# Loading each expert's weights as eight sets of one or two chunks in place of twelve transfers

## The reference, cut to what matters

```python
def moe(h, router_w, router_b, w1, b1, w2, b2):        # h: [512, 1024]
    top_v, top_i = lax.top_k(h @ router_w + router_b, 4)   # 4 of 32 experts for each token
    top_w = jax.nn.softmax(top_v, axis=-1)
    ...
    def block_ffn(args):                                # a block of tokens of one expert
        tok, e = args
        z = h[tok] @ w1[e] + b1[e]                      # w1[e]: [1024, 2048] float32, 8 MB
        z_glu, z_lin = jnp.split(z, 2, axis=-1)
        ...                                             # clamps
        act = z_glu * jax.nn.sigmoid(1.702 * z_glu) * (z_lin + 1.0)
        return act @ w2[e] + b2[e]                      # w2[e]: [1024, 1024] float32, 4 MB
```

## Time and profile before

| | |
|---|---|
| median of 3 runs | 1591.79 us (1590.99 to 1595.43) |
| span of the profiled execution | 1584.0 us |
| what the median has beside that span | 7.8 us |
| TensorE busy | 1461.9 us, 92% of the span |
| VectorE, ScalarE, GpSimd busy | 46%, 16%, 13% |
| moved by DMA | 497.19 MB, mean 314 GB/s |
| expert weights | 384 transfers of 1 MB, 204 into `big_b`, 180 into `arena` |

### The profile page before, as it was taken

The page is one execution under the profiler, slowest core; times in us unless marked ns, Lnnn a source line. Parts: engine busy times, 40 slices in busy tenths (PEclk is TensorE's granted clock), DMA queues, the critical chain, the costliest instruction groups (busy, mean ns, idle before and its releaser), DMA issues.

```text
span 1584.0 us, 39651 instructions
## 1 busy us (share of the span) xinstructions
PE 1461.9 (92%) x14639; PEld 738.5 (47%) x14639; DVE 735.8 (46%) x2464; ACT 261.3 (16%) x467; POOL 210.6 (13%) x267
## 2 busy tenths in 40 slices
PE   5999999999896899999979999979899979999896
PEld 3658888888653333433323434323333424333232
DVE  4503877777638544443424434424343423434244
ACT  4402555555413200000000000000000000000001
POOL 1000000000051112111211111211121111212110
PEclk9999999999998999999989999979999979999798
DMA  9685211112577999998798999999799998998997
GB/s 388 192 265 148 62 54 53 53 53 57 172 306 274 358 413 407 412 415 347 301 415 339 408 417 417 414 414 417 321 417 416 417 414 321 410 417 344 413 400 295
DMA packets 130857, 497.19 MB, mean 314 GB/s; under 512 B 15356, under 2 KB 48476, under 8 KB 94892
## 3 DMA queue, kind: packets, MB, share of 16 engines
q1 hardware_dynamic: 122396, 479.93, 77.1%
q0 software_dynamic: 8256, 16.81, 2.8%
q10 hardware_dynamic: 176, 0.06, 0.0%
HBM read 484.92 MB, written 17.58 MB: 317 GB/s over the span
## 4 chain that ended last, share of the span: by engine, by line
PE 71%; DMA 15%; SPq 7%; DVE 4%; issue 1%; ACT 1%; ACTq 0%; DVEq 0%; POOLq 0%
PE ps L1838 28%; PE ps L1870 14%; DMA big_b<-in_moe_w 7%; PE ps L1541 6%; PE ps L1542 6%; PE ps L1543 6%; DMA arena<-in_moe_w 5%; SPq L431 4%; PE ps L1720 3%; SPq L425 2%; PE ps L1652 1%; PE ps L1564 1%; DMA arena<-in_final_g 1%; PE ps L1851 1%; PE ps L1666 1%
## 5 line engine op out<-in xcount | busy, mean ns | idle before, releaser
L1838 PE MATMUL ps<-arena,rows 128*32 128x512 f32 x2736 | 318.2, 602 | 26.7 <-DMA arena<-in_moe_w 20.1
L1838 PE MATMUL ps<-big_b,rows 128*32 128x512 f32 x2688 | 316.8, 607 | 21.8 <-DMA big_b<-in_moe_w 21.8
L886 ACT ACTIVATE rows<-ps 128x256 f32<-128x256 f32 x84 | 32.3, 385 | 977.0 <-issue 661.5
L1838 PEld LDWEIGHTS ps<-arena,rows 128*32 128x32 f32 x2736 | 86.8, 111 | 214.0 <-issue 159.2
L1838 PEld LDWEIGHTS ps<-big_b,rows 128*32 128x32 f32 x2688 | 85.5, 111 | 208.1 <-issue 153.3
L1870 PE MATMUL ps<-big_b,rows 128*32 128x256 f32 x2688 | 163.9, 395 | 8.1 <-DMA big_b<-in_moe_w 8.1
L1870 PE MATMUL ps<-arena,rows 128*32 128x256 f32 x2688 | 161.7, 392 | 9.3 <-DMA arena<-in_moe_w 8.5
L1434 DVE SCALAR_TENSOR_TENSOR y_sb<-ps,w_s,g_q 128x256 f32<-128x256 f32 x42 | 20.3, 484 | 261.0 <-PE ps L1870 261.0
L1434 DVE SCALAR_TENSOR_TENSOR rows<-ps,w_s,g_q 128x256 f32<-128x256 f32 x42 | 20.3, 484 | 256.8 <-PE ps L1870 256.8
L1870 PEld LDWEIGHTS ps<-big_b,rows 128*32 128x32 f32 x2688 | 84.2, 113 | 68.1 <-DMA big_b<-in_moe_w 12.9
L1870 PEld LDWEIGHTS ps<-arena,rows 128*32 128x32 f32 x2688 | 84.1, 112 | 67.0 <-DMA arena<-in_moe_w 13.0
(11 more groups left out here) (360 smaller groups left out, 1785.0 us busy)
## 6 DMA issues: line engine op xcount, KB each, us to landing
big_b<-in_moe_w SPq DMA_DIRECT2D x204, 1024.0 KB, 14.2
arena<-in_moe_w SPq DMA_DIRECT2D x180, 1024.0 KB, 15.4
ring_t<-in_hg_w_in SPq DMA_DIRECT2D x32, 512.0 KB, 3.9
ogT<-in_mod_w SPq DMA_DIRECT2D x16, 1024.0 KB, 5.0
arena<-yrows SPq DMA_DIRECT2D x8, 1024.0 KB, 12.6
x_sb<-in_x SPq DMA_DIRECT2D x2, 2048.0 KB, 7.9
arena<-in_hg_w_in SPq DMA_DIRECT2D x4, 1024.0 KB, 13.8
arena<-in_mod_c SPq DMA_DIRECT2D x4, 1024.0 KB, 19.7
```

The source lines that it names most:

```text
L1838: last = mm(bank[q * G:(q + 1) * G, :], XT[par][:, pos * G:(pos + 1) * G], w[:, :, q * NW:(q + 1) * NW], start=(pos == 0), stop=False)
```

## The change

The weights keep their size and their total, but lie otherwise in HBM. w1 of an expert is laid out in five sets: chunk 0, chunks 1 and 2, chunk 3, chunks 4 and 5, chunks 6 and 7. w2 is laid out in three sets: chunks 0 and 1, chunk 2, chunk 3. Within a set, what one partition gets is one run: 8 KB in a set of one chunk, 16 KB in a set of two. Before, a partition's run was 8 KB for w1 and 4 KB for w2 (two runs in each chunk). The host writes the weights in this order ahead of the launch. Each set is one transfer with one semaphore; TensorE waits ahead of a set's first chunk and not ahead of its second; SP issues a set when TensorE has used the last chunk of the old set. The two chunks of a set must stand side by side in SBUF, so `B1_AT` and `B2_AT` change.

```diff
+W1_SET = ((0, 1), (1, 3), (3, 4), (4, 6), (6, 8))
+W2_SET = ((0, 2), (2, 3), (3, 4))
...
-        B1_AT, B2_AT = (5, 6, 7, 10, 11, 2, 3, 4), (0, 1, 8, 9)
+        flat_b = big_b[:, :, :].rearrange("p s n -> p (s n)")
+        B1_AT, B2_AT = (5, 6, 7, 4, 10, 11, 2, 3), (0, 1, 9, 8)
...
-            def load_w1(par, e, pos):
-                sp.dma_start(w1_slot(par, pos), moe_w1[bass.ds(e * D + pos * P, P), :]
-                             ).then_inc(ld_w1[par][pos], 16)
...
+            def load_set(par, e, at_a, at_b, source, sems, first, last):
+
+                n = (last - first) * 2 * FF
+                to = arena[:, at_a:at_a + n] if par == 0 else flat_b[:, at_b * 2 * FF:at_b * 2 * FF + n]
+                rows = source.rearrange("(r a) n -> r (a n)", a=last - first) if last - first > 1 else source
+                sp.dma_start(to, rows[bass.ds(e * (source.shape[0] // E // (last - first)) + first * P // (last - first), P), :]
+                             ).then_inc(sems[par][first], 16)
...
-                    over_w1(0, AHEAD)
+                    over_w1(range(4))
                     with sp.If(new_next):
-                        for k in range(W2C):
-                            sp.wait_ge(S["w2_used"], i * (2 * W2C) + (par * W2C + k + 1))
-                            load_w2(1 - par, e_next, k)
+                        for j in range(3):
+                            sp.wait_ge(S["w2_used"], i * (2 * W2C) + (par * W2C + W2_SET[j][1]))
+                            load_w2(1 - par, e_next, j)
...
-                    over_w1(AHEAD, W1C)
+                    over_w1(range(4, 5))
...
-                pe.wait_ge(ld_w1[par][pos], count + 16 * (1 - par))
+                if pos in (0, 1, 3, 4, 6):
+                    pe.wait_ge(ld_w1[par][pos], count + 16 * (1 - par))
...
-                    pe.wait_ge(ld_w2[par][m], i * 16 + 32)
+                    if m != 1:
+                        pe.wait_ge(ld_w2[par][m], i * 16 + 32)
```

More of the change, by code:

```diff
@@ L422, in _, with load_w1, load_w2 @@
                 sp.dma_start(b_raw[part * E:(part + 1) * E, :], moe_b1).then_inc(S["ld_br"], 16)
-            def load_w1(par, e, pos):
-                sp.dma_start(w1_slot(par, pos), moe_w1[bass.ds(e * D + pos * P, P), :]
-                             ).then_inc(ld_w1[par][pos], 16)
[L428 to L432, removed]
+            def load_set(par, e, at_a, at_b, source, sems, first, last):
[4 more added lines that the diff above has]
+                             ).then_inc(sems[par][first], 16)
+            def load_w1(par, e, j):
+                first, last = W1_SET[j]
+                load_set(par, e, first * 2 * FF, B1_AT[first], moe_w1, ld_w1, first, last)
+            def load_w2(par, e, j):
+                first, last = W2_SET[j]
+                load_set(par, e, 16384 + first * 2 * D, B2_AT[first], moe_w2, ld_w2, first, last)
             def store(i):
@@ L438, in store @@
                 sp.dma_start(hrows[i * P:(i + 1) * P, :], x_sb[:, i, :]).then_inc(S["h_st"], 16)
-            for pos in (5, 6, 7, 1, 2):
-                load_w1(1, 1, pos)
+            for j in (4, 2, 1):
+                load_w1(1, 1, j)
             sp.wait_ge(S["a_ps"], H)
-            for pos in range(W1C // 2):
-                load_w1(0, 0, pos)
+            for j in range(3):
+                load_w1(0, 0, j)
             sp.wait_ge(S["o_ps"], H)
             sp.wait_ge(S["og_ok"], H)
-            for pos in range(W1C // 2, W1C):
-                load_w1(0, 0, pos)
+            for j in range(3, 5):
+                load_w1(0, 0, j)
             sp.wait_ge(S["bias_ok"], 1)
@@ L453, in _ @@
             sp.wait_ge(S["yo_ps"], 2 * LT)
-            for k in range(2):
-                load_w2(0, 0, k)
+            load_w2(0, 0, 0)
             store(LT - 1)
             sp.wait_ge(S["lg_ps"], LT)
-            for pos in range(3, 5):
-                load_w1(1, 1, pos)
-            load_w2(0, 0, 2)
+            load_w1(1, 1, 3)
+            load_w2(0, 0, 1)
             sp.wait_ge(S["h_st"], 16 * LT)
             sp.wait_ge(ld_xg[0], 16)
-            for k in range(2):
-                load_w2(1, 1, k)
+            load_w2(1, 1, 0)
             for n in range(2):
                 sp.wait_ge(frow[n], 16 * (LT // 2))
-            load_w2(1, 1, 3)
+            load_w2(1, 1, 1)
             sp.wait_ge(S["late_free"], 1)
-            load_w2(0, 0, 3)
+            load_w2(0, 0, 2)
             sp.wait_ge(S["ring_free"], 1)
@@ L1942 @@
           "router_w": [D, E], "router_b": [E], "moe_w1": [E * D, 2 * FF], "moe_b1": [E, 2 * FF],
-          "moe_w2": [E * FF, D], "moe_b2": [E, D]}
+          "moe_w2": [E * FF // 2, 2 * D], "moe_b2": [E, D]}
 def kernel(**inputs):
@@ L1956 @@
     for name, n in (("moe_w1", 2 * FF), ("moe_w2", D)):
-        laid[name] = np.asarray(inputs[name]).reshape(E, QT, DK, G, n).transpose(0, 2, 1, 3, 4)
+        a = np.asarray(inputs[name]).reshape(E, QT, DK, G, n).transpose(0, 2, 1, 3, 4).reshape(E, DK, P, n)
+        sets, per = (W1_SET, 1) if name == "moe_w1" else (W2_SET, 2)
+        laid[name] = np.concatenate([a[:, first * per:last * per].transpose(0, 2, 1, 3).reshape(E, -1)
+                                     for first, last in sets], axis=1)
     for name in INPUTS:
```

21 lines of the change are left out of this document (11 added, 10 removed).

## The result

The changed kernel takes 1595.47 us in the median of 20 runs (1591.76 to 1600.06), the kernel before 1591.39 us (20 runs, 1584.41 to 1597.49). The ratio is 1.0033, 95% interval 1.0021 to 1.0045: **slower by a third of a per cent, where 0.44% faster was forecast.** 1595.47 us lies inside the range, at its far end. A second set of twelve runs gave 1.0029 (1.0010 to 1.0047).

A forecast was written before the change was run, and what follows sets the result against it. Bound: mostly TensorE's products, plus late weights in episodes paced by the DMA queue. Gains of 9.2 us, less 1.0 for half clock and 1.2 for gathers, gave 7.0 us: 1584.8 us, 0.44% faster; range 1578 to 1596 us.

The forecast's parts named there:

- Longer runs: Weight loads in the DMA queue: runs of 8 and 16 KB save 0.48 us a load, 1.6%.
- the list: Expert-stage episodes between queue dry points: gains of 1.4, 1.05, 3.85, 2.4, 0, 0, and 0.5 at the end, together 9.2 us.
- Coarser waits: TensorE's stalls ending on a set's second chunk: 0.86 us later each, plus 0.5 us for half clock at two places.
- Coarser release: SP's issue of a set of two comes 0.86 us later, but the queue holds over 2 us of work: no cost.
- The gathers at the start: Two token gathers on the chain at the start: held longer by longer runs, 0.6 us each, 1.2 us in all.
- The time around the span: Time of a run outside the profiled span: 7.8 us, which the change doesn't touch.
- Fewer instructions: Four TensorE waits fewer a block, four SP transfers fewer a load: no gain, though SP had 7% of the chain.
- the undisturbed block: A block of the expert stage in which TensorE doesn't wait: should still cost 10.87 us.
- no gain in pace: Rival on the weight loads: only 0.24 us or 0 saved a load, counted as no change; chance 0.30.
- zero case: Part of the no-gain rival: run length saves 0 us a load, giving 1594 to 1596 us; chance 0.12.
- its sign: What would show no gain in pace: in a stall, a set of two takes 4.98 us or more.
- Late gathers: Rival on block gathers: landing up to 9.5 us against 8.1 of room, 84 us lost, 1669 us; chance 0.10.

The follow-up runs named there:

- both edits: TensorE's waits and SP's releases go by the eight sets, still twelve 1 MB transfers, against w2 in 8 KB runs; ratio to before 1.0050 (1.0029 to 1.0071).

## Why the prediction was wrong

The pace came as predicted; the step that failed is the price of the coarse sets, waits and release together: 5.3 us in the sum, 13 us measured (both edits over w2 in 8 KB runs). A second one is what the pace was to give in time. The terms in their order:

- *Longer runs*, 0.48 us a load: right where the queue is dense. A set of two took 4.89 us (1505.90 to 1510.79 above; 4.92 predicted), a single w2 2.48. What a packet pays whatever its length is 11 to 12 ns by the medians above (two of 8 KB less one of 16, two of 4 less one of 8), where 7.5 was taken. The Trainium skill's "DMA: Bandwidth & Descriptors" (Specifications), by which 4 and 8 KB would run alike, is not borne out between those two, by 0.07 us a MB. But the list turned 1.6% of pace into 9.2 us net of 4.3 us for the coarse waits, so **13.5 us gross, which failed too**: measured is 3.3 us for the step to 8 KB and 0.4 to 4.1 us for that to 16 KB, behind the first blocks, where one kernel's two profiles lie as far apart. Over long stretches of full queue the changed kernel moved 0 to 1% more, not 1.6%.
- *Coarser waits*: **the step that failed, in the size of its term.** 0.86 us at each end on a set, and 0.5 for the clock at two places, 5.3 us in all; every such wait had a lowered clock behind it (0.50 in most, 0.62 at the highest measured), 1.9 us each, and coarse waits alone cost 7.6 us by the times. The ends on w2 chunk 3, where nothing was to be lost, became ends on chunk 7 (at 840.92, 1072.73 and 1301.37 us).
- *Coarser release*: costed at nothing, since "the queue always holds over 2 us of work". It does not: at six starts of a load the rate fell by 18 GB/s over 12 us. **This term, put at nothing, failed as well**: 5.4 us by the times on top of coarse waits, 2.4 without them, where the intervals overlap.
- *The gathers at the start*: 1.2 us taken, some 3 measured (4.4 less the 1.4 that before itself varies by). The third gather itself came 1.7 to 2.0 us later than in before, inside the bound of 3.4; the rest is the lowered clock behind it, which the sum left out.
- *The time around the span*: 1.8 us, not 7.8. It moved no difference, but the forecast mixed a lucky span with the median of other runs.
- *Fewer instructions* and the undisturbed block were right: 10.87 us a block still, and SP's share of the chain fell to 0% with no gain.

Of the rivals, *no gain in pace* with its zero case gave 1594 to 1596 us, and the measured 1595.47 lies there by luck: its sign, a set of two in 4.98 us or more, did not come (4.89). Late gathers through the whole stage did not come either: the median of a gather is 7.1 us in the changed kernel, its maximum 8.1 (8.3 in the second profile), against 8.1 of room. The estimate beside the rule of turns between queues in the Trainium skill's "DMA: Bandwidth & Descriptors" (Queues, rings and completion order), some 0.9 us more, met the 1.0 us measured. Tile of the gathers' numbers in the changed kernel (the earlier trace rows before):

```profile
DMA to landing us min/median/max: 2.7/7.1/8.1
```

No kernel here was slower than before by longer runs alone, and the best by its ratio is the change's smallest part: w2 in runs of 8 KB with twelve transfers, 1587.27 and 1587.93 us.

What stays open: how much time a run of 16 KB saves by itself, since a transfer of 2 MB brings the coarse wait and release with it (a packet of it is 1.9% shorter than two of 8 KB); why the price of single stalls doesn't add up; and what sets the clock between 428 and 456 us.

## What to carry to other kernels

Lay a tile out as one long run if that is free, but don't pay for it with coarser waits: where a consumer already waits for its loads, the work that is left behind the last landing is what counts, and it is priced at the clock that the longer idle time leaves. Release and load in pieces as small as those that the consumer uses, above all at the start of a load, where the queue is thinnest. And compare profiles from a common event onwards, with a second profile of each kernel, before explaining a few us.

## What was not expected of the hardware

TensorE's granted clock was 0.50 for the whole 3.64 us behind 4.2 to 4.7 us without products, and 1.00 or 0.53 behind idle times of 1.6 us. A gather that shares the queues with runs of 16 KB landed 1.0 us later in the median than with runs of 8 KB, while w2 in runs of 4 or 8 KB gave the same 6.0 to 6.1 us. The w2 chunk came 3% faster in runs of 8 KB than of 4 KB (2.48 against 2.55 us), and a packet of 16 KB took 611 ns where two of 8 KB took 622.
